# A decoder trunk's first stage reordered: second chunk later, units 0 and 1 row by row on both chunks, V's first tiles among the rows

## The chip, the cores and the metric

The kernel runs on one core of one Trainium2 chip. Five engines work from their own instruction queues: TensorE (PE, matmuls; its weight loads are PEld), VectorE (DVE), ScalarE (ACT), GpSimd (POOL) and SyncE (SP, here the issuer of most DMAs). Time is device microseconds of one execution; lower is better.

## The reference

One decoder layer for a prompt of 1024 tokens and 8 sample tokens, model width 1024, and a final norm, all in float32:

```python
mod = silu(c) @ w_ada + b_ada                       # (B, 6*D): sh1, sc1, gt1, sh2, sc2, gt2
h = rmsnorm(x, norm1_g) * (1.0 + sc1) + sh1
proj = h @ w_in                                     # xr, gr, q, k, v, o, ig, fg, u
# RG-LRU on xr, mLSTM on q k v ig fg, window pooling on u, each gated -> y_a, y_b, y_c
x = x + gt1 * (concat(y_a, y_b, y_c) @ w_out)
h2 = rmsnorm(x, norm2_g) * (1.0 + sc2) + sh2
x = x + gt2 * (square(relu(h2 @ w_ff1)) @ w_ff2)    # then the final rmsnorm
```

The change touches only the beginning: the conditioning (`mod`, of which `sh1` and `sc1` are needed first), the first norm, and the first products of `h` with `w_in`.

## The kernel before, in words

Tokens lie along the free axis. The 1032 tokens are cut into three chunks c of 344, the width 1024 into eight rows kt of 128. Float32 products are made of three fast ones: every operand is split into an upper part (`hi`, rounded by ACT) and a lower part (`lo`, the difference, made by POOL or VectorE), and TensorE adds hi\*hi, lo\*hi and hi\*lo. So each row of a 128-wide unit on one chunk is three matmuls (L2407 to L2409), a unit of eight rows 24.

`MIX_ORDER` is a text of steps, written out by hand. Every engine walks through the same list (`for s in plan`) and does its own share of each step in that order, with semaphores between the engines. So a step's place in the text sets its place on every engine that has a share in it. The steps at issue:

- `ADA:i:h`: half h of conditioning pair i (two tiles of 128 columns of `w_ada`; pieces of 512 KB that pass through four slots `RAWW`). TensorE multiplies (L2378, 8 matmuls); behind the second half ACT copies the result to `ADS` (L1297), before which it waits for the previous pair's ADT.
- `ADT:i`: TensorE turns the pair (L2392, 4 matmuls). `ADM:i`: VectorE adds the bias into `MOD` (L1717), and for the scale pairs (4 to 7) multiplies (L1719). Pair k gives the shift and pair 4+k the scale of rows 2k and 2k+1.
- `SQ:c:p`: ACT squares four rows of chunk c into two buffers (L1278), VectorE adds each to `SS` (L1763).
- `NS:c`: TensorE sums the squares over partitions (L2398, 2 matmuls), ACT takes the root (L1257), VectorE the reciprocal (L1742).
- `N:c:kt`: the normalised row. VectorE multiplies (L1728); for kt from `SHIFTED` on it adds the shift too (L1732) and ACT makes one copy to `H_hi` (L1239); for smaller kt ACT adds the shift in two operations (L1251, L1252). POOL makes `H_lo` (L1087).
- `W:u`: the weights of unit u: ACT the upper part (L1234), POOL the lower (L1082). Units 0 to 2 have early places `WR`.
- `DK:u:c:a:b`: TensorE's rows a to b-1 of unit u on chunk c, each row behind its own N. `D:u:c` for units 0 and 1 is only ACT's copy of the result.
- `WV:j`: a quarter of V's weights (784 elements a partition): ACT the upper part (L1282), VectorE the lower (L1777). `V:t`: TensorE's 24 matmuls of V on 128 tokens (L2434 to L2436), VectorE's copies (L1785, L1786); the first waits for all four WV.
- `R:n`: a DMA issue on ACT's queue.

SP issues the conditioning pieces in order (n = 0, 1, ...), the piece n behind the use of piece n-4; `SP_AFTER` says behind which piece the chunks of x (x1, x2), the early weights (w0, w1, w2) and V's weights (wv) are asked for. All through, transfers are served roughly in the order of their issue.

`bank_uses` gives each small result a PSUM bank: NS:1 had X2, which V:1 uses too.

Of the kernel before, what the change touches and what calls it, by code (L numbers as in the profile page):

```python
# [63 lines left out]
POOL_FIN = 2  # L64
POOL_STORED = (4, 6)
N_SP_RAW = 2 * len(ADA_START) + RAW
SP_AFTER = {3: ("x1",), 10: ("w1", "w0",), 16: ("wv",), 17: ("w2",), 18: ("x2",)}
N_EARLY_W = 3
R0 = NADA - N_EARLY_W


# [16 lines left out]
def unit_of(kind, t):  # L88
# [1 line left out]


MIX_ORDER = """
ADA:0:0 ADA:0:1 SQ:0:0 ADA:4:0 ADA:4:1 SQ:0:1 SQ:1:0 ADT:0 ADM:0 ADA:1:0 SQ:1:1 ADA:1:1 ADT:4 ADM:4 NS:0
ADA:5:0 ADA:5:1 N:0:0 ADT:1 ADM:1 N:0:1 ADA:2:0 ADA:2:1 ADT:5 ADM:5 ADA:6:0 ADA:6:1 ADT:2 ADM:2 N:0:2 ADA:3:0 W:0
    ADA:3:1 ADT:6 N:0:3 W:1 ADM:6 ADA:7:0 ADA:7:1 ADT:3 N:0:4 N:0:5 ADM:3 ADT:7 ADM:7 N:0:6 N:0:7 NS:1
DK:0:0:0:6
WV:0 DK:1:0:0:6
DK:0:0:6:8
WV:1 WV:2 DK:1:0:6:8
ADA:8:0  # L100
D:0:0 WV:3
D:1:0 N:1:0 N:1:1 N:1:2 N:1:3 N:1:4 V:0 SQ:2:0 DK:0:1:0:1
DK:1:1:0:1
DK:0:1:1:2
N:1:5 DK:1:1:1:2
DK:0:1:2:3
N:1:6 N:1:7 DK:1:1:2:3
DK:0:1:3:4
DK:1:1:3:4
SQ:2:1 DK:0:1:4:5  # L110
DK:1:1:4:5
R:20 ADA:8:1 DK:0:1:5:6
V:1 DK:1:1:5:6
NS:2
ADT:8 DK:0:1:6:7
DK:1:1:6:7
DK:0:1:7:8
V:2 DK:1:1:7:8
D:0:1
D:1:1 N:2:8 N:2:0 R:21 N:2:1 N:2:2 N:2:3 N:2:4 N:2:5 N:2:6 V:3 V:4 ADM:8 DK:0:2:0:8  # L120
N:2:7 W:2 V:5
D:0:2 R:22 DK:1:2:0:8
ADA:9:0 ADA:9:1 R:23 V:6 V:7 W:3 V:8 R:25 ADT:9
D:1:2 ADM:9 ADA:10:0 G1 ADA:10:1
# [73 lines left out]
def bank_uses(plan):  # L198

    count = {b: 0 for b in AUX}  # L200
    use = {}

    def add(key, bank):
        use[key] = (bank, count[bank])
        count[bank] += 1

    for s in plan:
        k = s[0]
        if k == "NS":
            add(s, ("X0", "X2", "X0")[s[1]])  # L210
        elif k == "V":
            add(s, ("X1", "X2")[s[1] % 2])
        elif k == "ADA" and s[2] == 0:
            add(("ADA", s[1]), "X3" if s[1] in ADA_START[::2] else "X4")
        elif k == "ADT":
            add(s, "X1" if s[1] in ADA_START else "X4" if s[1] == NPAIR - 1 else "X3")
        elif k in ("G1", "G2", "G3", "G4", "Y", "YS"):
            add(s, "X3")
        elif k == "TS":
            for w in range(2):  # L220
                add(("TS", w), ("X3", "X4")[w])
        elif k == "LRUG":
            for g in range(2):
                for c in range(NCH):
                    add((*s, g, c), ("X0", "X1", "X2")[c])
        elif k == "S":
            add(("S", s[1]), "X0")
            add(("KT", s[1]), "X3")
        elif k == "AB":
            add(("A", s[1]), "X1")  # L230
            add(("B", s[1]), "X2")
        elif k == "U":
            add(s, "X0")
# [56 lines left out]
def build(nc, I, O):  # L290
# [24 lines left out]
    with ExitStack() as ctx:  # L315
# [762 lines left out]
        def _(pool):  # L1078
# [25 lines left out]
            for s in plan:  # L1104
                k = s[0]
                if k == "W":
                    if s[1] < N_EARLY_W:
                        w_lo(s[1], None, s[1] % 2, WR[s[1]])
                    else:
                        w_lo(s[1], raw_slot(s[1]), s[1] % 2)  # L1110
                elif k == "N":
                    lo(full_at[s], *views(s))
                elif k == "D":
                    if s in full_at:
                        lo(full_at[s], *views(s))
                elif k in ("YD", "YSD"):
                    if k == "YD" and s[1] == 0:
                        pool.wait_ge(s_out, 32)
                    key = (k[:-1], *s[1:])
                    lo(full_at[key], *views(key))  # L1120
                elif k == "POOLY":
                    key = ("POOL", *s[1:])
                    lo(full_at[key], *views(key))
                elif s == ("POOLV", 0):

                    pool.wait_ge(h_ready, LRU_T)
                    for c in range(NCH):
# [85 lines left out]
        def _(act):  # L1213
# [30 lines left out]

            def hi_norm(n, hi_v, lo_v, fu_v, shift, kt):

                if kt >= SHIFTED:
                    hi(n, hi_v, fu_v)
                else:
                    act.wait_ge(full_ready, n + 1)  # L1250
                    nc.scalar.activation(hi_v, fu_v, ACT.Identity, bias=MOD[:, shift + kt, 0:1])  # L1251
                    nc.scalar.activation(fu_v, fu_v, ACT.Identity, bias=MOD[:, shift + kt, 0:1]).then_inc(hi_ready, 1)  # L1252
# [424 lines left out]
        def _(dve):  # L1677
# [78 lines left out]
            for s in plan:  # L1756
# [1129 lines left out]
```

## Time and profile before

| | us |
|---|---|
| median of 3 runs | 1175.13 |
| range of the runs | 1174.47 to 1175.67 |
| the profiled execution | 1175.78 |
| its span | 1174.0 |
| TensorE busy | 1124.6 (96%) |
| VectorE busy | 792.8 (68%) |
| ACT busy | 473.4 (40%) |
| POOL busy | 346.9 (30%) |
| mean granted TensorE clock | 0.982 |

The page gives the span and each engine's busy time. In the timelines a row is: start in us, length in us, engine, line of the kernel, operation, output and inputs by the program's names (buffer numbers left out), form, count, and in brackets the idle time ahead of it and who ended it. Matmuls overlap in the pipeline: one of 344 columns is shown as 0.32 us long, but the next starts 0.157 us behind it at the full clock. The granted clock (PEclk) is 1.00 for 2.4 GHz and 0.50 for 1.2 GHz.

### The profile page before, as it was taken

Reading aid. Unit: us, or ns where it says so; the run is one execution under the profiler, and the core shown is the slowest. Engines: PE = TensorE matmul, PEld = TensorE weight load, DVE = VectorE, ACT = ScalarE, POOL = GpSimd, SP = SyncE. Lnnn points to the kernel's source line nnn. Section 1 sums busy time; section 2 is a strip of 40 time slices with the busy share of each in tenths; the row PEclk is TensorE's granted clock in tenths of the full one; section 3 lists DMA queues with packets and bytes.
Section 4 is the critical chain, followed back from the end, with each engine's and each line's share of the span. In section 5 each row is a group of like instructions: output and inputs, shape, how many; then the busy total and the mean of one; then the engine's idle time right before and its main releaser. Section 6 shows DMA issues by size and latency. Waiting matters only on the chain.

```text
span 1174.0 us, 19681 instructions
## 1 busy us (share of the span) xinstructions
PE 1124.6 (96%) x7237; PEld 1077.3 (92%) x7237; DVE 792.8 (68%) x1319; ACT 473.4 (40%) x780; POOL 346.9 (30%) x275
## 2 busy tenths in 40 slices
PE   4799999999989999999999999999999999999997
PEld 1598888888979999899999999999999999999996
DVE  4561455478775434678578878778778788788546
ACT  5551355655456344642233332332432433433431
POOL 0442011201434357764032022132131231231352
PEclk9699999998989999999999999999999999999998
DMA  8912523566523722111111111202102202111104
GB/s 302 326 57 88 142 90 126 177 180 218 176 87 113 269 90 73 54 55 37 37 36 55 54 37 55 71 18 71 56 16 75 68 18 72 53 50 58 37 1 145
DMA packets 67846, 109.85 MB, mean 94 GB/s; under 512 B 6435, under 2 KB 42567, under 8 KB 67399
## 3 DMA queue, kind: packets, MB, share of 16 engines
q1 hardware_dynamic: 57574, 84.88, 22.0%
q10 hardware_dynamic: 10208, 24.12, 6.6%
q8 instruction: 41, 0.67, 0.2%
q14 instruction: 23, 0.18, 0.0%
HBM read 96.81 MB, written 12.18 MB: 93 GB/s over the span
## 4 chain that ended last, share of the span: by engine, by line
PE 82%; DVE 9%; ACT 3%; DMA 2%; issue 1%; POOL 1%; SPq 1%; ACTq 0%; POOLq 0%; DVEq 0%
PE D L2407 7%; PE D L2409 7%; PE D L2408 7%; PE D L2591 6%; PE D L2593 5%; PE D L2592 5%; PE X L2593 5%; PE X L2591 5%; PE X L2592 5%; PE X L2663 5%; PE X L2664 5%; PE X L2665 5%; PE D L2663 2%; PE D L2665 2%; PE D L2664 2%; DMA RAWW<-in_WADA 2%
## 5 line engine op out<-in xcount | busy, mean ns | idle before, releaser
L2407 PE MATMUL D<-H_hi,W_hi 128*128 128x344 f32 x472 | 158.6, 336 | 3.7 <-POOL H_lo L1087 3.1
L2409 PE MATMUL D<-H_hi,W_lo 128*128 128x344 f32 x472 | 152.4, 323 | 0.0
L2408 PE MATMUL D<-H_lo,W_hi 128*128 128x344 f32 x472 | 152.4, 323 | 0.0
L1087 POOL TENSOR_TENSOR Y_lo<-FU,Y_hi 128x344 fp32r<-128x344 f32 (+3 forms) x84 | 100.1, 1194 | 154.2 <-ACT Y_hi L1521 88.5
L1082 POOL TENSOR_TENSOR W_lo<-RAWW,W_hi 128x1024 fp32r<-128x1024 f32 x25 | 61.6, 2465 | 182.5 <-ACT W_hi L1234 182.2
L1087 POOL TENSOR_TENSOR Y_lo<-EY,Y_hi 128x344 fp32r<-128x344 f32 (+1 forms) x24 | 38.3, 1598 | 216.3 <-ACT Y_hi L1521 144.5
L2407 PEld LDWEIGHTS D<-H_hi,W_hi 128*128 128x128 f32 x472 | 90.5, 192 | 11.8 <-issue 7.6
L2408 PEld LDWEIGHTS D<-H_lo,W_hi 128*128 128x128 f32 x472 | 90.3, 191 | 0.9 <-issue 0.5
L2409 PEld LDWEIGHTS D<-H_hi,W_lo 128*128 128x128 f32 x472 | 90.2, 191 | 0.0
L2215 DVE SCALAR_TENSOR_TENSOR X<-X,MOD 128x344 f32<-128x344 f32 (+1 forms) x138 | 75.7, 566 | 9.2 <-PE X L2665 9.0
L2663 PE MATMUL X<-Y_hi,W_hi 128*128 128x344 f32 x252 | 80.7, 320 | 0.0
L2664 PE MATMUL X<-Y_lo,W_hi 128*128 128x344 f32 x252 | 80.6, 320 | 0.0
L2665 PE MATMUL X<-Y_hi,W_lo 128*128 128x344 f32 x252 | 80.5, 319 | 0.0
L2017 DVE SCALAR_TENSOR_TENSOR X<-D,MOD,X 128x344 f32<-128x344 f32 (+1 forms) x72 | 41.3, 573 | 45.4 <-PE D L2593 24.7
L2407 PE MATMUL D<-Y_hi,W_hi 128*128 128x344 f32 x192 | 62.0, 323 | 1.5 <-POOL W_lo L1082 1.5
L1099 POOL TENSOR_TENSOR SS<-SS,SQ 128x344 f32<-128x344 f32 x45 | 43.3, 963 | 65.9 <-ACT SQ L1430 40.5
L1087 POOL TENSOR_TENSOR Y_lo<-KEPT,Y_hi 128x344 fp32r<-128x344 f32 x24 | 26.4, 1098 | 120.7 <-ACT Y_hi L1521 120.7
L2408 PE MATMUL D<-Y_lo,W_hi 128*128 128x344 f32 x192 | 61.3, 319 | 0.0
L2409 PE MATMUL D<-Y_hi,W_lo 128*128 128x344 f32 x192 | 61.3, 319 | 0.0
L1556 ACT ACTIVATE W_hi<-RAWW 128x1024 fp32r<-128x1024 f32 x30 | 31.8, 1059 | 64.3 <-PE X L2665 55.6
L2378 PE MATMUL X<-RAWW,CTX 128*32 128x256 f32 x384 | 35.7, 461 | 19.5 <-DMA RAWW<-in_WADA 19.4
L1087 POOL TENSOR_TENSOR H_lo<-FU,H_hi 128x344 fp32r<-128x344 f32 (+2 forms) x33 | 29.9, 914 | 66.2 <-ACT FU L1252 50.7
(416 smaller groups left out, 3455.1 us busy)
## 6 DMA issues: line engine op xcount, KB each, us to landing
RAWW<-in_W SPq DMA_DIRECT2D x76, 512.0 KB, 3.6
RAWW<-in_WADA ACTq DMA_DIRECT2D x28, 512.0 KB, 4.1
RAWW<-in_WADA SPq DMA_DIRECT2D x20, 512.0 KB, 8.0
RAWW<-in_W ACTq DMA_DIRECT2D x18, 512.0 KB, 3.7
X0T<-in_x SPq DMA_DIRECT2D x3, 1376.0 KB, 12.8
out_y<-OUTN SPq DMA_DIRECT2D x24, 172.0 KB
X<-in_x SPq DMA_DIRECT2D x8, 344.0 KB, 5.3
NM<-nm_d SPq DMA_DIRECT2D x8, 256.0 KB, 5.3
```

The source lines that it names most:

```text
L1082: nc.gpsimd.tensor_tensor(lo_v, RAWW[:, raw, :] if src is None else src[:], hi_v.bitcast(F32), ALU.subtract).then_inc(w_lo_ready, 1)
L1087: nc.gpsimd.tensor_tensor(lo_v, fu_v, hi_v.bitcast(F32), ALU.subtract).then_inc(lo_ready, 1)
L2215: V.scalar_tensor_tensor(out=X[:, m, c * CH:c * CH + w], in0=ps[:, 0:w], scalar=MOD[:, 5 * KT + m, 0:1], in1=X[:, m, c * CH:c * CH + w], o ...
L2407: T.matmul(out, w_h, hi[:, kt, a:b], start=(kt == 0), stop=False)
L2408: T.matmul(out, w_h, lo[:, kt, a:b], start=False, stop=False)
L2409: one = T.matmul(out, w_l, hi[:, kt, a:b], start=False, stop=(kt == KT - 1))
L2591: T.matmul(out, w_h, hi(kt), start=(kt == 0 and not onto), stop=False, skip_group_check=onto)
L2592: T.matmul(out, w_h, lo(kt), start=False, stop=False, skip_group_check=onto)
L2593: one = T.matmul(out, w_l, hi(kt), start=False, stop=(kt == n - 1), skip_group_check=onto)
L2663: T.matmul(bank[:, 0:CH], w_hi[:, a:a + P], h, start=(start and k == 0), stop=False, skip_group_check=onto)
L2664: T.matmul(bank[:, 0:CH], w_hi[:, a:a + P], l, start=False, stop=False, skip_group_check=onto)
L2665: one = T.matmul(bank[:, 0:CH], w_lo[:, a:a + P], h, start=False, stop=(stop and k == 1), skip_group_check=onto)
```

## The change

The order of the first stage is rewritten; the amount of work is the same.

```diff
-SP_AFTER = {3: ("x1",), 10: ("w1", "w0",), 16: ("wv",), 17: ("w2",), 18: ("x2",)}
+SP_AFTER = {5: ("w0",), 7: ("w1",), 9: ("x1",), 15: ("wv",), 17: ("x2",), 18: ("w2",)}
 N_EARLY_W = 3
+N_DVE_W = 2
...
-ADA:0:0 ADA:0:1 SQ:0:0 ADA:4:0 ADA:4:1 SQ:0:1 SQ:1:0 ADT:0 ADM:0 ADA:1:0 SQ:1:1 ADA:1:1 ADT:4 ADM:4 NS:0
-ADA:5:0 ADA:5:1 N:0:0 ADT:1 ADM:1 N:0:1 ADA:2:0 ADA:2:1 ADT:5 ADM:5 ADA:6:0 ADA:6:1 ADT:2 ADM:2 N:0:2 ADA:3:0 W:0
-    ADA:3:1 ADT:6 N:0:3 W:1 ADM:6 ADA:7:0 ADA:7:1 ADT:3 N:0:4 N:0:5 ADM:3 ADT:7 ADM:7 N:0:6 N:0:7 NS:1
-DK:0:0:0:6
-WV:0 DK:1:0:0:6
-DK:0:0:6:8
-WV:1 WV:2 DK:1:0:6:8
-ADA:8:0
-D:0:0 WV:3
-D:1:0 N:1:0 N:1:1 N:1:2 N:1:3 N:1:4 V:0 SQ:2:0 DK:0:1:0:1
+ADA:0:0 ADA:0:1 SQ:0:0 ADA:4:0 ADT:0 ADM:0 ADA:4:1 SQ:0:1 ADA:1:0 ADT:4 ADM:4 NS:0 ADA:1:1 W:0 N:0:0 N:0:1 ADA:5:0 ADT:1 ADM:1
+ADA:5:1 W:1 ADA:2:0 ADT:5 ADM:5 DK:0:0:0:2 N:0:2 N:0:3 ADA:2:1 DK:1:0:0:2 ADA:6:0 ADT:2 ADM:2 ADA:6:1 DK:0:0:2:4
+    ADA:3:0 ADT:6 ADM:6 N:0:4 N:0:5 SQ:1:0 DK:1:0:2:4 ADA:3:1 ADA:7:0 ADT:3 ADM:3 SQ:1:1 DK:0:0:4:6 ADA:7:1 ADT:7 ADM:7 N:0:6 N:0:7 DK:1:0:4:6 NS:1
+DK:0:0:6:7
+DK:1:0:6:7 N:1:0
+DK:0:0:7:8 N:1:1
+DK:1:0:7:8
+D:0:0 WV:0
+D:1:0 N:1:2 WV:1 ADA:8:0 DK:0:1:0:1
 DK:1:1:0:1
-DK:0:1:1:2
-N:1:5 DK:1:1:1:2
-DK:0:1:2:3
-N:1:6 N:1:7 DK:1:1:2:3
-DK:0:1:3:4
+N:1:3 WV:2 DK:0:1:1:2
+DK:1:1:1:2
+N:1:4 WV:3 DK:0:1:2:3
+DK:1:1:2:3
+N:1:5 V:0 DK:0:1:3:4
 DK:1:1:3:4
-SQ:2:1 DK:0:1:4:5
+N:1:6 DK:0:1:4:5
 DK:1:1:4:5
+N:1:7 V:1
 R:20 ADA:8:1 DK:0:1:5:6
-V:1 DK:1:1:5:6
-NS:2
-ADT:8 DK:0:1:6:7
+SQ:2:0 DK:1:1:5:6
+DK:0:1:6:7
 DK:1:1:6:7
-DK:0:1:7:8
-V:2 DK:1:1:7:8
-D:0:1
-D:1:1 N:2:8 N:2:0 R:21 N:2:1 N:2:2 N:2:3 N:2:4 N:2:5 N:2:6 V:3 V:4 ADM:8 DK:0:2:0:8
-N:2:7 W:2 V:5
+SQ:2:1 DK:0:1:7:8
+DK:1:1:7:8
+D:0:1 ADT:8
+D:1:1 V:2 NS:2 N:2:8 N:2:0 R:21 N:2:1 N:2:2 V:3 N:2:3 N:2:4 N:2:5 N:2:6 V:4 N:2:7 ADM:8 DK:0:2:0:8
+W:2 V:5
...
-            add(s, ("X0", "X2", "X0")[s[1]])
+            add(s, ("X0", "X3", "X0")[s[1]])
...
-    SHIFTED = KT - 2
+    SHIFTED = ((1, 3, 5, 7, KT), (KT - 2, KT - 1, KT))
...
-                    if s[1] < N_EARLY_W:
+                    if s[1] < N_DVE_W:
+                        pass
+                    elif s[1] < N_EARLY_W:
...
-                if kt >= SHIFTED:
+                if kt in SHIFTED[shift > 0]:
...
-                    if kt >= SHIFTED:
+                    if kt in SHIFTED[shift > 0]:
...
+                elif k == "W" and s[1] < N_DVE_W:
+                    u = s[1]
+                    dve.wait_ge(w_hi_ready, u + 1)
+                    V.tensor_tensor(W_lo[:, u, :], WR[u][:], W_hi[:, u, :].bitcast(F32), ALU.subtract).then_inc(w_lo_ready, 1)
```

In words: x1 is asked for behind piece 9 instead of piece 3, w0 and w1 behind pieces 5 and 7, wv behind 15. Units 0 and 1 take chunk 0's rows in pairs between the conditioning pieces and chunk 1's rows one by one. V:0 stands before row 3 of chunk 1, V:1 before row 5, V:2 behind the chunk; the four WV stand between the N steps of chunk 1. The lower parts of W:0 and W:1 move from POOL to VectorE. In the first norm the odd rows, not rows 6 and 7, have their shift on VectorE. NS:1 gets bank X3.

## Rows read from the trace of the kernel before

**Rows 1.** The page, busy time and share of the span by engine.
```profile
PE 1124.6 (96%) x7237; PEld 1077.3 (92%) x7237; DVE 792.8 (68%) x1319; ACT 473.4 (40%) x780; POOL 346.9 (30%) x275
```
**Rows 2.** TensorE by stretches: stretch, us, busy (instructions), granted clock, DMA share, GB/s.
```profile
0.00:46.08 46.08, 24.33 (x164) 0.82 0.88 310
...
61.62:66.35 4.73, 4.73 (x31) 1.00 0.12 42
66.35:80.80 14.45, 13.05 (x81) 1.00 0.14 51
81.00:1174.00 1093.00, 1067.53 (x6883) 0.99 0.26 83
```
**Rows 3.** TensorE's waits, 0 to 81 us: total, times, longest.
```profile
PE X L2378 <- DMA RAWW<-in_WADA: 19.4, 8, 10.4
```
**Rows 4.** TensorE's timeline.
```profile
22.23 0.99 PE L2392 MATMUL X<-SEL,ADS 128*128 128x9 f32 x4 [0.34 <-DVE MOD L1717]
23.07 1.49 PE L2398 MATMUL X<-SS,ONE 128*128 128x344 f32 x2
...
35.68 1.08 PE L2378 MATMUL X<-RAWW,CTX 128*32 128x256 f32 x8 [4.77 <-DMA RAWW<-in_WADA]
...
47.45 0.49 PE L2407 MATMUL D<-H_hi,W_hi 128*128 128x344 f32 x1
47.74 0.49 PE L2408 MATMUL D<-H_lo,W_hi 128*128 128x344 f32 x1
...
55.57 0.32 PE L2409 MATMUL D<-H_hi,W_lo 128*128 128x344 f32 x1
57.24 0.45 PE L2434 MATMUL X<-WV_hi,H_hi 128*128 128x392 f32 x1 [0.78 <-DVE WV_lo L1777]
...
69.01 0.34 PE L2434 MATMUL X<-WV_hi,H_hi 128*128 128x392 f32 x1
...
73.24 0.32 PE L2407 MATMUL D<-H_hi,W_hi 128*128 128x344 f32 x1
```
**Rows 5.** ACT's timeline.
```profile
25.29 0.55 ACT L1257 ACTIVATE SS<-X,EPT 128x344 f32<-128x344 f32 x1
...
39.60 1.04 ACT L1234 ACTIVATE W_hi<-WR 128x1024 fp32r<-128x1024 f32 x1
...
49.19 2.34 ACT L1282 ACTIVATE WV_hi<-WV_raw 128x784 fp32r<-128x784 f32 x3
54.98 0.46 ACT L1322 ACTIVATE ST<-D 128x344 f32<-128x344 f32 x1 [3.45 <-PE D L2409]
...
57.71 0.58 ACT L1251 ACTIVATE H_hi<-FU,MOD 128x344 fp32r<-128x344 f32 x1 [1.18 <-DVE FU L1728]
...
58.67 0.57 ACT L1251 ACTIVATE H_hi<-FU,MOD 128x344 fp32r<-128x344 f32 x1
```
**Rows 6.** VectorE's timeline.
```profile
17.28 2.21 DVE L1763 TENSOR_TENSOR SS<-SS,SQ 128x344 f32<-128x344 f32 x4 [1.35 <-ACT SQ L1278]
...
41.13 1.99 DVE L1719 SCALAR_TENSOR_TENSOR MOD<-MOD,COLS 128x18 f32<-128x18 f32 x1
...
46.34 0.57 DVE L1728 SCALAR_TENSOR_TENSOR FU<-X0T,MOD,X 128x344 f32<-128x344 f32 x1
...
47.27 0.57 DVE L1728 SCALAR_TENSOR_TENSOR FU<-X0T,MOD,X 128x344 f32<-128x344 f32 x1
...
49.32 2.31 DVE L1742 RECIPROCAL X<-SS 128x344 f32<-128x344 f32 x1 [0.99 <-ACT SS L1257]
...
56.21 0.98 DVE L1777 TENSOR_TENSOR WV_lo<-WV_raw,WV_hi 128x784 fp32r<-128x784 f32 x1 [1.80 <-ACT WV_hi L1282]
...
63.07 2.57 DVE L1763 TENSOR_TENSOR SS<-SS,SQ 128x344 f32<-128x344 f32 x4 [0.48 <-ACT SQ L1278]
```
**Rows 7.** POOL's timeline.
```profile
40.72 2.37 POOL L1082 TENSOR_TENSOR W_lo<-WR,W_hi 128x1024 fp32r<-128x1024 f32 x1
...
58.85 4.72 POOL L1087 TENSOR_TENSOR H_lo<-FU,H_hi 128x344 fp32r<-128x344 f32 x5 [8.86 <-ACT FU L1252]
```

## The prediction

> **What bounds the kernel now.** I read the page's busy shares first: TensorE is busy 1124.6 of 1174.0 us [rows 1], so time can only come out of its idle time, of what it runs at the half clock, or be lost as new idle time. The stretches come next [rows 2]: up to 46.08 us TensorE is busy 24.3 us, with the DMA queues at 0.88 of their share (the conditioning weights stream in); from 57.24 on it is busy nearly all the time at the granted clock 1.00. Past 81 us nothing of the order changes and TensorE works 1067.5 of 1093 us, so what the first 81 us lose or gain goes through to the end almost one to one. Of TensorE's waits in these 81 us 19.4 us are for conditioning pieces [rows 3]; for V's weights it waits 0.78 us, ahead of V:0 [rows 4]. The timelines [rows 4 to 7] give the durations. I use one marker: at 80.80 us before, TensorE has finished units 0 and 1 on chunks 0 and 1, V:0 to V:2, both halves of ADA:8, ADT:8 and NS:2. The new order contains the same work up to a point behind D:1:1; I ask when that point comes.
>
> **Part 1, the start up to NS:0 (gain about 4 us, hidden later).** Before, ADT:4 waited for ADM:0, which VectorE did behind chunk 1's first squares (the row at 22.23, [rows 4]); NS:0 followed at 23.07. Chunk 0's squares were summed at 17.28 + 2.21 = 19.5 [rows 6]. With ADM:0 ahead of SQ:0:1, and chunk 1's squares gone, NS:0 starts at 19.5 and takes 1.4; the root 0.55 [rows 5] and the reciprocal 2.31 [rows 6] end at 23.9, where before the root began at 25.29 and the reciprocal ended at 28.2. Asking for x1 six pieces later moves 1.41 MB, at 310/0.88 = 352 GB/s [rows 2] 4.0 us of the queues, but the bytes ahead of the last piece (ADA:7:1) are the same, so I take nothing from that by itself.
>
> **Part 2, chunk 0 among the pieces (over at about 51 us, before at 55.9, [rows 4]).** All engines follow the same order, so each pair of rows waits for a chain: piece, ACT's copy, ADT, ADM, N, ACT, POOL.
> - Rows 0 and 1: W:0's low part on VectorE, 0.98 x 1024/784 = 1.27 us (estimate from the 784-wide row in [rows 6]), 23.9 to 25.2; N:0:0 0.5, N:0:1 0.93 with its shift (46.34 to 47.27 in [rows 6]): 26.6. ACT 0.55 behind, POOL 0.92 each (4.72/5, [rows 7]): first dense row on TensorE at 28.7.
> - Rows 2 and 3: ACT's copy for ADA:5 0.4 and W:1's upper part 1.04 [rows 5] end at 28.6; VectorE's W:1 1.27, ADM:5 0.4, two N 1.43: 31.7. ACT is free for ADA:2's copy at 32.3, done at 32.7.
> - TensorE from 28.7: at the half clock a DK of two rows is 6 x 0.287 = 1.72 (47.45 to 47.74, [rows 4]), a piece 1.0 to 1.08, an ADT 1.0. DK, ADA:2:1, DK end at 33.1. Wide matmuls take most of this stretch, as in the one before the clock's rise at 50 us, so I let the clock be full from about 33. Then ADA:6:0, ADT:2, ADA:6:1, DK, ADA:3:0, ADT:6 at half those durations: 3.6, so 36.7.
> - ADM:6 0.4, N:0:4 and N:0:5 1.43, ACT 0.55: 39.3. Now ACT does SQ:1:0 before it copies ADA:3, and SQ:1:1 before it copies ADA:7. Four squares with their sums take 2.21, and 2.57 where POOL works on rows beside them (17.28 and 63.07, [rows 6]); I take 2.6. 39.3 + 2.6 + 0.4 + 2.6 + 0.4 = 45.3. ADT:7 0.7, ADM:7 0.4, two N 1.45, ACT 0.5, root 0.55, reciprocal 2.35: chunk 1's reciprocal ends at 51.3.
>
> Call that moment T; before it was 49.32 + 2.31 = 51.6 [rows 6]. So T hardly moves, though chunk 0's dense work is over by then. Bounds: with the full clock from 28.7, ADT:2 is held by ACT's copy at 32.7 and T is 50.0. With the half clock throughout, TensorE needs 6 x 1.72 + 7 x 1.0 + 4 x 1.0 + 1.4 = 22.7 us from 28.7 and some 0.7 of waits, and T is 52.1 + 0.55 + 2.35 = 55.0. I take 51.4.
>
> **Part 3, V's weights split between the rows (the loss).** Before, WV:0 to WV:2 stood together on ACT (2.34 for three) and on VectorE, and ran under the 9.8 us of chunk 0's dense work (46.1 to 55.9); only WV:3 waited (for the ACT copy of D:0:0 at 54.98), and V:0 started at 57.24 [rows 4 to 6]. Now the order on ACT and on VectorE alike is WV:0, N:1:2, WV:1, N:1:3, WV:2, N:1:4, WV:3. A WV goes from ACT to VectorE and an N from VectorE to ACT. So ACT can't start WV:1 before VectorE has done N:1:2, and VectorE can't start N:1:3 before ACT has done WV:1. Nothing overlaps. One round is WV on ACT 0.78 (2.34/3), 0.12, WV on VectorE 0.98, N on VectorE 0.5 or 0.93, 0.1, N on ACT 0.96 or 0.47 (57.71 to 58.67 in [rows 5]; a shifted row is the single copy): 3.4 us. From T: N:1:0 to ACT and its two ACT operations 1.6, N:1:1 on ACT 0.47, D:0:0's copy 0.4, WV:0 0.78, that is 3.25; three rounds to WV:3's ACT part, 10.2; 0.12 + 0.98. V:0 may start at T + 14.6 = 66.0.
>
> Until then TensorE has ADA:8:0 and three double rows of chunk 1, 6 x 0.157 = 0.94 each (4.73/30, [rows 2]), and stands behind V:0, which comes before row 3. It is idle from about 59 to 66, and sparsely used from 51 on. So the cover that is gone is chunk 0's dense work: it was over V's weights and chunk 1's normalising, and has been spent on the piece waits.
>
> From V:0 to the marker: three V tiles at 73.24 - 69.01 = 4.23 [rows 4], 12.7; five double rows, 4.7; and the rest of the stretch 66.35 to 80.80, 13.05 - 8.46 - 18 x 0.157 = 1.8 (ADA:8:1, ADT:8, NS:2). Sum 19.2. Row 7 of chunk 1 and SQ:2 are done while V:1 runs, so no wait there. 66.0 + 19.2 = 85.2.
>
> **Part 4, the clock behind the hole.** Before, the dense work began at 46.1 and still ran at half speed at 47.7 (0.29 us a matmul against 0.157, [rows 2, 4]); about twelve of its matmuls were slow, which cost 12 x 0.13 = 1.6 us. Behind an idle stretch of 7 us V:0 will start at half speed as well: 0 to 2.5 us, I take 1.7.
>
> **Part 5, chunk 2.** NS:2 now stands behind V:2. V:3 and V:4 (8.5 us) cover 12.5 us of root, reciprocal and nine rows at POOL's 0.92 less 3.3 us of dense rows in progress: 0.3 us more wait than before, 0 to 1.0.
>
> **Part 6, W:0 and W:1 off POOL, odd shifts on VectorE.** The MOD operation that takes 0.2 us otherwise took 1.99 while POOL's 2.37 us W operation ran, and ended with it [rows 6, 7]. That goes, and is in T. The 4.7 us of POOL were otherwise not on the path. The odd shifts make a row 0.47 on ACT and 0.93 on VectorE where it was 0.96 and 0.5: in a serial round that is nothing. The same row says that VectorE's WV operations, which now fall among POOL's row operations, can be held by them: at worst 0.92 each, 3.7 for four. In the round above POOL's row operation starts together with ACT's WV of 0.78 and is nearly over when VectorE's turn comes, so the sum takes nothing and the worst is a rival.
> The Trainium skill, "SBUF — State Buffer", section "Who interferes with whom", says that a VectorE operation with two SBUF inputs and a GpSimd operation that reads SBUF lock each other out for a whole instruction, whichever is issued first. By that each of the three rounds grows by the end of POOL's operation that overlaps, some 0.2 us, and the sum by 0.6; by the row alone it could be nothing or all of it.
>
> **Sum.** 85.2 + 1.7 + 0.3 = 87.2 against 80.8: +6.4 us, I say +6.2, since a little may be taken up by later waits. The profiled execution took 1175.78 us (span 1174.0), 0.65 over the median of 1175.13. So 1182.0 for such an execution, 1181.3 for a median. Own range: T 50.0, no clock cost: 64.6 + 19.2 = 83.8, +3.0; T 55.0 with 2.5 and 1.0: 69.6 + 19.2 + 3.5 = 92.3, +11.5, which all three bounds rarely reach together. 1178 to 1186.5.
>
> **Rivals.**
> - Faster: the rows fill the piece waits and chunk 1's chain comes forward with NS:0. Chunk 0's 9.5 us shrink to its last two double rows at 1.9: -7.6 us, +1.0 for a late first row of chunk 1, so 1175.1 - 6.6 = 1168.5. For it speaks that 19.4 us of piece waits are there to be filled, and that NS:0 comes 4.4 us sooner. Against it: V:0 would have to start before 66.0 - 6.2 = 59.8, T + 14.6 says T at 45.2, and the two square groups on ACT between ADA:3 and ADA:7 alone put ADT:7 behind 45. 0.10.
> - No change: the hole behind T is only as long as what was saved, which asks for T near 45. 1175.1. 0.04.
> - The lock of part 6 or a late clock makes it worse: POOL's operations hold each WV by 0.92, 1181.3 + 3.7 = 1185.0. 0.06.
> - That the second chunk, asked for late, holds SQ:1:0: it would have to land after 39; with the pieces before it, it lands near 30. It is in none of the sums, under 0.01.
>
> My forecast holds 0.80. Faster by over 0.2% 0.10, within 0.2% (2.3 us, about what a measurement of this kernel can tell from none) 0.04, slower 0.86. The range is stretched downward to 1176 for the part between.
>
> **What would show it.** NS:0's reciprocal ends near 24, the one of NS:1 near 51. On VectorE and ACT WV and N alternate with about 3.4 us from one WV to the next. TensorE waits some 6 to 7 us for WV_lo ahead of V:0 at about 66, with the clock at 0.5 in this stretch; the marker stands at 87. It is wrong if NS:1's reciprocal ends by 46, or if WV:3's low part is done by 60.

## The result and the profile after

The changed kernel takes 1184.0 us (median of 7 runs, 1182.6 to 1188.06), the one before 1175.47 beside it (7 runs, 1172.84 to 1179.29). The ratio is 1.0087, 95% interval 1.0067 to 1.0107: slower by 0.9%. Forecast was 1181.3 in a range of 1176.0 to 1186.5.

| | before | after |
|---|---|---|
| profiled execution, us | 1175.78 | 1184.0 |
| its span | 1174.0 | 1182.2 |
| TensorE busy | 1124.6 | 1124.8 |
| mean granted clock | 0.982 | 0.983 |
| chunk 1's reciprocal ends (T) | 51.63 | 54.69 |
| V:0 starts | 57.24 | 69.18 |
| marker: V:0 to V:2, both units on two chunks, NS:2 done | 80.80 | 90.38 |
| second marker, see below | 116.92 | 127.85 |

TensorE is as busy as before over the whole span; what is new is idle time. The page of the kernel after, busy time by engine (answers to [rows 1]):

```profile
PE 1124.8 (95%) x7237; PEld 1076.3 (91%) x7237; DVE 794.3 (67%) x1327; ACT 470.5 (40%) x774; POOL 341.9 (29%) x273
```

TensorE by stretches (stretch, us, busy, granted clock, DMA share, GB/s; answers to [rows 2]):

```profile
42.00:52.50 10.50, 8.52 (x32) 0.53 1.02 381
52.50:62.50 10.00, 5.42 (x36) 0.98 0.23 80
62.50:73.00 10.50, 4.29 (x16) 0.53 0.01 2
73.00:90.38 17.38, 17.38 (x107) 0.99 0.15 54
```

Two stretches ran at half speed (1.2 GHz), and from 52.5 to 73.0 TensorE did only 9.7 us of work. Before, the corresponding time behind T was nearly full: 17.8 of the 20 us from 52 to 72. TensorE's waits in the first 100 us (waiting tile, releaser, total, times, longest; answers to [rows 3]):

```profile
PE X L2384 <- DMA RAWW<-in_WADA: 12.9, 6, 10.1
PE X L2440 <- DVE WV_lo L1783: 6.2, 1, 6.2
PE X L2398 <- ACT ADS L1299: 5.9, 3, 3.8
PE D L2413 <- POOL H_lo L1087: 4.8, 3, 2.4
PE X L2404 <- DVE SS L1765: 0.9, 1, 0.9
```

The piece waits did shrink, from 19.4 to 12.9 us, but 6.2 us for V's weights (0.8 before), 5.9 for ACT's copies (none before) and 4.8 for chunk rows (1.8 before) have come instead. TensorE's timeline (answers to [rows 4]):

```profile
19.08 1.51 PE L2404 MATMUL X<-SS,ONE 128*128 128x344 f32 x2 [0.94 <-DVE SS L1765]
...
43.15 1.02 PE L2398 MATMUL X<-SEL,ADS 128*128 128x9 f32 x4 [3.78 <-ACT ADS L1299]
44.02 0.63 PE L2413 MATMUL D<-H_hi,W_hi 128*128 128x344 f32 x1
...
46.02 1.08 PE L2384 MATMUL X<-RAWW,CTX 128*32 128x256 f32 x8
47.67 1.02 PE L2398 MATMUL X<-SEL,ADS 128*128 128x9 f32 x4 [0.56 <-ACT ADS L1299]
...
50.41 1.35 PE L2404 MATMUL X<-SS,ONE 128*128 128x344 f32 x2
...
57.52 0.40 PE L2413 MATMUL D<-H_hi,W_hi 128*128 128x344 f32 x1 [2.43 <-POOL H_lo L1087]
61.79 0.40 PE L2413 MATMUL D<-H_hi,W_hi 128*128 128x344 f32 x1 [2.15 <-POOL H_lo L1087]
69.18 0.69 PE L2440 MATMUL X<-WV_hi,H_hi 128*128 128x392 f32 x1 [6.21 <-DVE WV_lo L1783]
...
73.27 0.37 PE L2440 MATMUL X<-WV_hi,H_hi 128*128 128x392 f32 x1
...
104.02 0.43 PE L2413 MATMUL D<-H_hi,W_hi 128*128 128x344 f32 x1 [0.94 <-POOL H_lo L1087]
```

In VectorE's timeline (answers to [rows 6]) the four WV operations stand apart, each behind a wait for ACT's part, and N operations between them (the third, at 64.70, is left out):

```profile
52.38 2.31 DVE L1744 RECIPROCAL X<-SS 128x344 f32<-128x344 f32 x1 [1.66 <-ACT SS L1259]
...
57.88 1.20 DVE L1783 TENSOR_TENSOR WV_lo<-WV_raw,WV_hi 128x784 fp32r<-128x784 f32 x1 [1.67 <-ACT WV_hi L1284]
61.43 1.04 DVE L1783 TENSOR_TENSOR WV_lo<-WV_raw,WV_hi 128x784 fp32r<-128x784 f32 x1 [1.87 <-ACT WV_hi L1284]
...
68.09 1.04 DVE L1783 TENSOR_TENSOR WV_lo<-WV_raw,WV_hi 128x784 fp32r<-128x784 f32 x1 [1.87 <-ACT WV_hi L1284]
```

The chain of waits that ended last shows the same as one thread (start, us, what). One round, from N:1:2 to WV:1:

```profile
59.08 0.49 DVE FU L1730
59.58 0.03 issue
59.60 0.58 ACT H_hi L1253
60.19 0.47 ACT FU L1254
60.66 0.76 ACT WV_hi L1284
61.41 0.02 issue
61.43 1.04 DVE WV_lo L1783
```

No piece of it lies on two engines at once. The waits in the timelines say the same: VectorE stood 1.87 us for ACT ahead of its operation at 61.43 (above), and ACT stood 1.41 us for VectorE ahead of its own at 59.60:

```profile
59.60 0.58 ACT L1253 ACTIVATE H_hi<-FU,MOD 128x344 fp32r<-128x344 f32 x1 [1.41 <-DVE FU L1730]
```

That is the round of part 3.

### The profile page after: what moved, and what is told of

Its sections match the earlier page's. It is cut to its first block, busy times and chain, and to the rows that moved or that the text cites. A ratio compares the mean times of both kernels' runs of the same rounds, so it can differ in the third digit from the quotient of the medians.

```text
span 1182.2 us, 19690 instructions
## 1 busy us (share of the span) xinstructions
PE 1124.8 (95%) x7237; PEld 1076.3 (91%) x7237; DVE 794.3 (67%) x1327; ACT 470.5 (40%) x774; POOL 341.9 (29%) x273
## 4 chain that ended last, share of the span: by engine, by line
PE 80%; DVE 10%; ACT 3%; DMA 3%; issue 1%; POOL 1%; SPq 1%; POOLq 0%; ACTq 0%; DVEq 0%
PE D L2413 7%; PE D L2415 6%; PE D L2414 6%; PE D L2597 6%; PE D L2599 5%; PE D L2598 5%; PE X L2599 5%; PE X L2597 5%; PE X L2598 5%; PE X L2669 5%; PE X L2671 5%; PE X L2670 5%; PE D L2669 2%; PE D L2671 2%; PE D L2670 2%; DMA RAWW<-in_WADA 2%
## 5 line engine op out<-in xcount | busy, mean ns | idle before, releaser
L1082 POOL TENSOR_TENSOR W_lo<-RAWW,W_hi 128x1024 fp32r<-128x1024 f32 x25 | 61.3, 2452 | 179.7 <-ACT W_hi L1236 179.3
L2413 PEld LDWEIGHTS D<-H_hi,W_hi 128*128 128x128 f32 x472 | 90.5, 192 | 19.2 <-issue 13.7
L2414 PE MATMUL D<-Y_lo,W_hi 128*128 128x344 f32 x192 | 61.3, 319 | 0.0
L2415 PE MATMUL D<-Y_hi,W_lo 128*128 128x344 f32 x192 | 61.3, 319 | 0.0
L1558 ACT ACTIVATE W_hi<-RAWW 128x1024 fp32r<-128x1024 f32 x30 | 31.7, 1058 | 63.9 <-PE X L2671 55.3
L2671 PEld LDWEIGHTS X<-Y_hi,W_lo 128*128 128x128 f32 x252 | 47.4, 188 | 0.0
```

Of the source, the lines that this page charges most:

```text
L1082: nc.gpsimd.tensor_tensor(lo_v, RAWW[:, raw, :] if src is None else src[:], hi_v.bitcast(F32), ALU.subtract).then_inc(w_lo_ready, 1)
L2413: T.matmul(out, w_h, hi[:, kt, a:b], start=(kt == 0), stop=False)
L2414: T.matmul(out, w_h, lo[:, kt, a:b], start=False, stop=False)
L2415: one = T.matmul(out, w_l, hi[:, kt, a:b], start=False, stop=(kt == KT - 1))
L2671: one = T.matmul(bank[:, 0:CH], w_lo[:, a:a + P], h, start=False, stop=(stop and k == 1), skip_group_check=onto)
```

## How the experiments are read

The executions of one kernel differ by 2 to 9 us, so besides the timed ratio I use a place in the order that every kernel has: the first matmul that turns V's gate columns (`X<-IDN,GTE`), which stands behind all that the change moves. It is the second marker of the table, 116.92 us before and 127.85 after (+10.9). Its row in TensorE's timeline, in the kernel before:

```profile
116.92 0.27 PE L2458 MATMUL X<-IDN,GTE 128*36 128x128 f32 x1 [0.29 <-DVE MOD L1717]
```

In the kernel after:

```profile
127.85 0.27 PE L2464 MATMUL X<-IDN,GTE 128*36 128x128 f32 x1 [0.29 <-DVE MOD L1719]
```

The kernel before was profiled a second time (before_again):

> The kernel before, unchanged, profiled once more. It tells how far one trace of a kernel stands from another. Theory (the first stage is the same from execution to execution within 2 us, which is set by where the clock rises, and the spread of the times comes from the half-clock stretches between 240 and 365 us): matmul 1200 starts within 2 us of 214.4 and the rest of the span differs by 0 to 4 us with the half-clock time. Rival (the first stage itself varies by 3 us or more): the differences of 4 us that the experiments' traces show would not be safe.

There the marker is at 116.43, 0.5 us from the first profile, although the whole execution took 1178.25 us instead of 1175.78. The kernel both, profiled twice, had it 0.9 us apart. So the first stage repeats better than the total, but a difference of 1 to 2 us at the marker, which rests on one trace on either side, is only a little more than that. Three of the recorded expectations speak of matmul 1200 of the trace instead; it stands at 214.4 us in the kernel before and moves as the marker does (10.9 us later in the kernel after). All kernels, in us:

| kernel | T | marker, against before | span, against before | ratio to before | 95% |
|---|---|---|---|---|---|
| after | 54.7 | +10.9 | +8.2 | 1.0087 | 1.0067 to 1.0107 |
| wv_together | 54.3 | +6.7 | +10.2 | 1.0076 | 1.0052 to 1.0100 |
| v_behind_rows | 55.0 | +9.6 | +9.5 | 1.0083 | 1.0064 to 1.0101 |
| squares_early | 50.1 | +6.0 | +4.7 | 1.0052 | 1.0033 to 1.0070 |
| both | 50.1 | +2.7 | +5.9 | 1.0063 | 1.0044 to 1.0083 |
| both_again (one execution) | 51.4 | +3.6 | +7.1 | | |
| x1_early | 56.2 | +13.4 | +10.4 | 1.0111 | 1.0084 to 1.0139 |
| w_on_pool | 55.1 | +12.5 | +15.9 | 1.0080 | 1.0055 to 1.0105 |
| before_dve_w | 53.5 | +2.2 | +0.2 | 1.0032 | 1.0016 to 1.0047 |
| covered | 53.5 | -4.0 | -5.4 | 0.9959 | 0.9944 to 0.9974 |
| covered_wv14 | 53.3 | -4.1 | +1.1 | 0.9949 | 0.9929 to 0.9969 |
| rows_late | 51.5 | -2.3 | -0.5 | 1.0004 | 0.9987 to 1.0021 |
| before_again (one execution) | 50.8 | -0.5 | +2.4 | | |

## The experiments

**wv_together.** The changed kernel with V's weights in one piece.

```diff
-D:0:0 WV:0
-D:1:0 N:1:2 WV:1 ADA:8:0 DK:0:1:0:1
+D:0:0 WV:0 WV:1 WV:2 WV:3
+D:1:0 N:1:2 ADA:8:0 DK:0:1:0:1
 (and WV:2, WV:3 gone from behind N:1:3 and N:1:4)
```

> The changed kernel with its four WV steps together behind D:0:0, where only WV:0 stood; all else as changed. Theory (serial rounds): T, the end of chunk 1's reciprocal, stays at 54.7. ACT does four WV in a row from 57.0 (0.78 each), VectorE follows with the last at about 61.1 to 62.0, then N:1:2. TensorE waits for row 2 of chunk 1 until about 64.3 and goes straight on to V:0 there, instead of 69.2: 4.9 us less, and up to 1.5 more because the clock has less idle time to fall in. Ratio to the kernel before about 1.003 instead of 1.0087. Rival (V's weights are late for another reason, their transfer or POOL's hold on VectorE): V:0 still starts at 68 to 69 and the time is that of the changed kernel.

VectorE's timeline of wv_together, where the four now run back to back:

```profile
57.45 3.85 DVE L1783 TENSOR_TENSOR WV_lo<-WV_raw,WV_hi 128x784 fp32r<-128x784 f32 x4 [1.67 <-ACT WV_hi L1284]
```

They are done at 61.3 instead of 69.1; V:0 starts at 65.86 and waits for nothing, TensorE's longest wait is 3.8 us for a row of chunk 1 instead of 6.2 for the weights. The marker comes 4.2 us sooner than in the kernel after. So the serial rounds are a cause, and one edit of the order on ACT and VectorE takes 4.2 of the 10.9 us away. The total doesn't show it: 1.0076, which is 1.3 us under the changed kernel's 1.0087 and inside both intervals. Where the rest went is taken up in the part on the total below.

**v_behind_rows.** V:0 moved behind row 4 of chunk 1, so that TensorE meets it later.

```diff
-N:1:5 V:0 DK:0:1:3:4
+N:1:5 DK:0:1:3:4
...
-N:1:7 V:1
+V:0 N:1:7 V:1
```

> The changed kernel with V:0 behind row 4 of chunk 1 on all engines instead of ahead of row 3; the WV stay between the N. Theory (serial rounds): rows 3 and 4 come no faster than one per 3.4 us (ready at 64.9 and 68.3), so they only fill the wait: V:0 starts at about 69.3 as before, two double rows of 0.94 are already done, 1.9 us less, perhaps 1 more by the clock. Ratio 1.006 to 1.007. Rival (V:0's place ahead of the rows makes the loss, the rows are ready): TensorE's wait of 6.2 us goes altogether and the ratio is 1.003 or less.

The marker is 1.3 us sooner, against the 1.9 and perhaps 1 more that were expected. WV_lo starts at 58.22, 61.77, 65.03 and 68.42, 3.3 to 3.6 us apart as in the kernel after: TensorE's order has no part in the rounds. It only decides how many rows are used to fill the hole, and there are few to be had, since the rows' own N operations stand in the same rounds.

**squares_early.** Chunk 1's squares before the last pieces instead of between them.

```diff
-... ADT:2 ADM:2 ADA:6:1 DK:0:0:2:4
-    ADA:3:0 ADT:6 ADM:6 N:0:4 N:0:5 SQ:1:0 DK:1:0:2:4 ADA:3:1 ADA:7:0 ADT:3 ADM:3 SQ:1:1 ...
+... ADT:2 SQ:1:0 ADM:2 ADA:6:1 DK:0:0:2:4 SQ:1:1
+    ADA:3:0 ADT:6 ADM:6 N:0:4 N:0:5 DK:1:0:2:4 ADA:3:1 ADA:7:0 ADT:3 ADM:3 ...
```

> The changed kernel with SQ:1:0 ahead of ADM:2 and SQ:1:1 ahead of ADA:3:0, so chunk 1's squares lie in ACT's and VectorE's idle time at 32 to 38 us. Theory (T is set by the squares between ACT's copies of ADA:3 and ADA:7): ADT:3 starts at about 41 instead of 43.15, ADM:7 ends at 45 to 46 instead of 49.2, T is 50 to 51.5 instead of 54.7, V:0 starts 14.5 later at 65 to 66: 3 to 4 us less, ratio 1.005. Rival (the clock or the pieces set T): T stays within 1 us of 54.7.

TensorE and VectorE of squares_early:

```profile
41.03 0.61 PE L2398 MATMUL X<-SEL,ADS 128*128 128x9 f32 x4 [1.77 <-ACT ADS L1299]
...
64.57 0.69 PE L2440 MATMUL X<-WV_hi,H_hi 128*128 128x392 f32 x1 [5.33 <-DVE WV_lo L1783]
```
```profile
47.77 2.31 DVE L1744 RECIPROCAL X<-SS 128x344 f32<-128x344 f32 x1 [1.01 <-ACT SS L1259]
```

ADT:3 waits 1.77 us instead of 3.78 for ACT's copy, the clock stays at 1.00 from 42 to 52 us, where the kernel after had 0.53, and T is 50.08, 4.6 sooner. V:0 starts at T + 14.5, as in the kernel after. The marker is 5.0 sooner, more than the 3 to 4 expected, and the time follows it (1.0052). That the edit keeps the clock full is not shown: see both_again.

**both.** The two edits together, timed, and **both_again**, the same kernel profiled a second time.

> The changed kernel with the edits of wv_together and squares_early at once. Each took 4.2 and 4.9 us off the stage (matmul 1200 of the trace came 10.9 us later than before in the changed kernel, 6.7 and 6.0 later in these two). Theory (serial rounds and T are two losses one behind the other): they add up, 10.9 - 4.2 - 4.9 = 1.8 us later than before, ratio 1.000 to 1.004. Rival (both took off the same idle time): 5 us or more later, 1.005.

> The kernel both, unchanged, profiled once more. Its trace showed the stage 2.7 us longer than before, but its times were 7.4 us longer. Theory (clock): matmul 1200 again 1 to 4 us later than the kernel before; the rest is half-clock time behind 240 us, which differs from execution to execution. Rival (the stage of that one trace was a lucky one): matmul 1200 comes 5 us or more later.

At the marker the edits roughly add up: -4.2 and -5.0 from +10.9 give +1.8, measured +2.7 and +3.6. The total doesn't: 1.0063 is 7.4 us, its interval (5.2 to 9.8 us) doesn't hold the marker's figure, and the ratio expected, at most 1.004, was missed.

The two profiles of this one kernel also price the clock by itself. TensorE from 42 to 52 us (columns as above), in both, then in both_again:

```profile
42.00:52.00 10.00, 6.45 (x45) 1.00 1.02 387
```
```profile
42.00:52.00 10.00, 9.17 (x35) 0.53 1.04 385
```

ADT:3 waited 1.76 us in the first and 1.61 us in the second; ADT:7 started at 44.11 and 44.40, NS:1 at 45.61 and 47.14, and T is 50.07 and 51.41. So the half clock in this stretch costs T 1.3 us, or 2.0 counted from ADT:3, which began at 41.02 and 40.37, and the same order gave it in one execution and not in the other. By this estimate 1.3 to 2.0 of the 4.6 us by which squares_early has T sooner are the clock, and the rest is the squares' place.

**x1_early.** The changed kernel with x1 asked for behind piece 3 again.

```diff
-SP_AFTER = {5: ("w0",), 7: ("w1",), 9: ("x1",), 15: ("wv",), ...
+SP_AFTER = {3: ("x1",), 5: ("w0",), 7: ("w1",), 15: ("wv",), ...
```

> The changed kernel with the second chunk of x asked for behind piece 3 as before; all else as changed. Theory: its 1.4 MB then stand ahead of pieces 4 to 9, ADA:1:0 starts at about 19.5 instead of 16.1, NS:0 behind it at about 21 instead of 19.1, and ADA:1:1 and all that follows some 2 to 3.5 us later: T at 57 to 58, the stage 2 to 3.5 us longer, ratio 1.011. Rival (the request's place is free, since the bytes ahead of the last piece are the same): stage within 0.5 us of the changed kernel.

Piece waits rise from 12.9 to 15.0 us, chunk 0's reciprocal ends at 25.90 instead of 23.59, and the marker is 2.5 us later (ratio 1.0111). So asking for the second chunk late is worth 2.5 us at the marker in this order: an early x1 holds the pieces in front of NS:0, where ADA:1:0 starts at 19.52 behind a wait of 3.44 us, instead of at 16.09. The timed ratios, 1.0111 and 1.0087, have intervals that overlap.

**w_on_pool** and **before_dve_w.** The lower parts of W:0 and W:1 back on POOL in the changed kernel (`N_DVE_W = 0`); and, alone, in the kernel before, moved to VectorE with the odd rows shifted there.

> The changed kernel with the lower parts of W:0 and W:1 back on POOL. In the kernel before, the move of these two to VectorE (with the odd shifts) made the stage 2.2 us longer. Theory (in the new order POOL is idle at 23 to 26 and 28 to 31, so it makes no difference where they run; N:0:0 starts 1.2 us sooner, ADM:5 is held until POOL's W ends, some 1 us later): stage within 1 us of the changed kernel, ratio to the kernel before 1.008 to 1.009. Rival (VectorE is too loaded and this is part of the loss): 2 us or more less, 1.007 or below.

> The kernel before with only two parts of the change: the lower parts of W:0 and W:1 on VectorE, and the odd rows of the first norm with their shift on VectorE. Theory: no share in the loss; the VectorE operation on MOD that took 1.99 us goes back to 0.2, the two W take 1.25 each there; time within 1 us of the kernel before (ratio 0.999 to 1.001). Rival (these parts cost: VectorE is loaded where it is on the path): 1.002 or more.

In the changed kernel POOL's version puts the marker 1.5 us later and the ratio (1.0080) can't be told from 1.0087. There VectorE's operation on MOD for ADM:5 takes 2.02 us again (at 28.10, beside POOL's operation for W:1). In the kernel before, VectorE's version, together with the odd shifts, costs 2.2 us at the marker and 0.32% in time, which I had not expected. VectorE of before_dve_w:

```profile
43.81 1.23 DVE L1780 TENSOR_TENSOR W_lo<-WR,W_hi 128x1024 fp32r<-128x1024 f32 x1 [1.50 <-ACT W_hi L1237]
44.95 0.17 DVE L1720 TENSOR_TENSOR MOD<-X,COLS 128x18 f32<-128x18 f32 x1
```

VectorE, which walks the order too, stands 2.07 us (at W:0) and 1.50 us (at W:1) waiting for ACT's upper part, and ADM:6 behind it comes at 44.95 instead of 40.92. It ends at 45.34, against 43.12 in the kernel before, where POOL's operation had stretched it: 2.2 us later, which is the figure at the marker. TensorE's next ADT waits 3.0 us for it. POOL could wait for ACT with nothing behind it. How much of the 2.2 us the odd shifts have was not tested apart. It is the same effect as in the rounds: an added hand-over stops everything that the receiver has further on.

**covered.** A version of my own: both squares early; WV:0 to WV:2 behind ADM:3 while chunk 0 is still being worked on, WV:3 behind NS:1, wv asked for behind piece 13; V:0 and V:1 right behind chunk 0's rows, ahead of chunk 1's dense rows. Further on NS:2 stands ahead of row 6, and V:2 to V:4 among chunk 2's N steps. It shows what these edits do together, not what each of them does.

```diff
-...ADA:7:0 ADT:3 ADM:3 SQ:1:1 DK:0:0:4:6 ADA:7:1...
-DK:1:0:6:7 N:1:0
-D:0:0 WV:0
-D:1:0 N:1:2 WV:1 ADA:8:0 DK:0:1:0:1
+...ADA:7:0 ADT:3 ADM:3 WV:0 WV:1 WV:2 DK:0:0:4:6 ADA:7:1...
+WV:3 DK:1:0:6:7 N:1:0
+D:0:0
+D:1:0 N:1:2 ADA:8:0 N:1:3 V:0 N:1:4 N:1:5 N:1:6 N:1:7 V:1 R:20
+DK:0:1:0:1 SQ:2:0
...
```

> The change's first part kept (chunk 0's rows among the pieces, second chunk late), and its losses taken away: chunk 1's squares in the idle time at 32 to 38 us, V's weights asked for behind piece 13 and split at 41 to 45 us (WV:0 to WV:2 behind ADM:3, WV:3 behind NS:1), V:0 and V:1 straight behind chunk 0's rows as cover while chunk 1 is normalised, NS:2 ahead of row 6, V:2 to V:4 as cover for chunk 2. Theory (the loss is serial rounds without cover plus T): chunk 0 done near 50, V:0 from 51, no wait for chunk 1's rows, the 450th matmul some 6 to 8 us sooner than before: 1167 to 1170, ratio 0.993 to 0.995. Rival (the opening is bound by its pieces, and chunk 0's rows among them gain nothing): no faster than the kernel before, ratio 1.00.

TensorE of covered:

```profile
41.28 0.79 PE L2385 MATMUL X<-RAWW,CTX 128*32 128x256 f32 x8 [3.44 <-DMA RAWW<-in_WADA]
...
54.60 0.45 PE L2441 MATMUL X<-WV_hi,H_hi 128*128 128x392 f32 x1 [0.61 <-DVE WV_lo L1784]
```

V:0 starts 14.6 us sooner than in the kernel after, at once at full speed (its matmuls stand 0.18 us apart), and covers chunk 1's eight rows. The marker is at -4.0 us and the kernel is faster than the kernel before and the kernel after, 0.9959 (0.9944 to 0.9974). The expectation was a few us better. I took the row at 41.28 for what is missing, and the next run tests that: the 1.6 MB of wv now stand ahead of ADA:7:0, TensorE waits 3.44 us for it and the clock falls to 0.51 until 52.

**covered_wv14.** The same with wv one piece later.

> The kernel covered with V's weights asked for behind piece 14 instead of 13. In covered TensorE waited 3.4 us for ADA:7:0 at 41.3, whose transfer stood behind the 1.6 MB of V's weights. Theory: the wait goes, chunk 1's reciprocal ends at 50 to 51 instead of 53.5, the stage is 2 to 3.5 us shorter than covered, 6 to 7.5 us shorter than before: 1167 to 1169, ratio 0.993 to 0.995. Rival (the wait only moves to ADA:7:1, one piece later): within 1 us of covered, 0.996.

TensorE of covered_wv14:

```profile
44.68 1.08 PE L2385 MATMUL X<-RAWW,CTX 128*32 128x256 f32 x8 [1.33 <-DMA RAWW<-in_WADA]
```

The wait for ADA:7:0 is 0.77, at 39.48, and one of 1.33 stands at ADA:7:1 instead; VectorE waits 2.54 us for V's upper parts. T and marker stay where they were (53.3, -4.1), where T at 50 to 51 was expected: the rival came true. The queues were at 1.05 of their share in this stretch: I take it that V's weights and the last two pieces have to come in before T in whatever order, which no run tests apart. The ratio is 0.9949 (0.9929 to 0.9969), not to be told from covered.

**rows_late.** covered_wv14 with chunk 0's dense rows all behind NS:1, as in the kernel before.

> The kernel covered_wv14 with chunk 0's twelve DK groups behind NS:1, in the pieces' order of the kernel before (0:6, 0:6, 6:8, 6:8), so nothing dense runs among the pieces. Theory (rows among the pieces save TensorE's time once V:0 and V:1 cover the rest): the pieces come sooner without them, the last dense row of chunk 0 ends at 54 to 57 instead of 52.6 and V:0 starts there instead of at 54.4: the stage 1 to 3 us longer than covered_wv14, ratio 0.996 to 0.998. Rival (they only take time from the chain of pieces): the same or less time, 0.995 or below.

T comes 1.9 us sooner (51.45), for no dense row at half speed stands before NS:1, but all 16 rows then follow it; the marker (114.64) is 1.9 us later than in covered_wv14 (112.78). So the rows among the pieces, the main idea of the change, are a gain of 1.9 us at the marker, if nothing is spoiled behind them. The ratio is 1.0004 where 0.996 to 0.998 was expected: timed, the two kernels are about 6.5 us apart (1.0004 against 0.9949, intervals that don't touch). The sign is the marker's; the other 4.6 us lie behind it and stay open, since the one profile of either kernel doesn't show them.

## Why the prediction was right, and where its numbers were off

The sign and the mechanism held, the price of the first stage was too low, and part of the agreement in the total is luck. At the first marker it had 87.2 and the trace has 90.38; at the second the kernel is 10.9 us late, where the sum said 6.4. By its steps:

- **Part 1 held.** NS:0 started at 19.08 (19.5 said), its reciprocal ended at 23.59 (23.9).
- **Part 2 was mis-sized, by 3.3 us: T is 54.69, not 51.4.** First row and N:0:2/3 came as said (28.00 for 28.7, 31.2 for 31.7), ADM:6 was done at 38.09 (36.7 + 0.4 = 37.1 said; the sum's next figure, 39.3, should by its own terms be 39.1). Then ADT:3 had to wait for a copy behind SQ:1:0 until 43.15 (42.3 said). The step that failed is the next one: I had added up only ACT's work from SQ:1:0 to ADT:7, and let the clock be full from 33. In those 3.78 us of waiting the clock fell to half (0.53 from 42.0 to 52.5), and ADA:7:1 stood behind a double row on TensorE that started at 44.02 and took 2.0 us, so that ADA:7:1 began at 46.02, ADT:7 at 47.67 and NS:1 at 50.41. From ADT:7's start (47.67, 45.3 said) that is 2.4 us; ADT:7 at half speed adds 0.4 and ACT's root, which had to wait for NS:1, 0.5. T lies just inside my bound of 55.0, which was made of just this, the half clock on TensorE's own chain. squares_early takes the wait from 3.78 to 1.77, had the full clock and gives T = 50.08, my lower bound of 50.0. How the 3.3 us divide between the order on ACT and the clock is not shown for this kernel; both and both_again put the clock at 1.3 to 2.0 us there.
- **Part 3 held.** V:0 started at T + 14.49 (14.6 said), with rounds of 3.55, 3.27 and 3.39 us (3.4 said) and a wait of 6.2 (6 to 7 said). wv_together removes the wait and 4.2 us; v_behind_rows leaves the rounds alone.
- **Part 4 held.** The clock was 0.53 from 62.5 to 73.0, and V:0's first 12 matmuls took 73.27 - 69.18 = 4.09 us instead of 12 x 0.176 = 2.1 [rows 4]: 2.0 us (1.7 said). From V:0 to the first marker 21.2 us passed (19.2 + 1.7 said).
- **Part 5 was mis-sized, by 1.0 us.** The row behind V:4 starts at 98.93, against 89.24 in the kernel before: +9.7. From V:5 at 104.60 against 93.64 it is +11.0. In between TensorE waits for chunk 2's last rows, the longest wait being 0.94 us at 104.02 (0.36 before). I had said 0.3, within 0 to 1.0; with the 0.3 it is 1.3, above that bound.
- **Part 6.** The VectorE operation that POOL's W operation had stretched to 1.99 us takes 0.18, as said, and W:0's lower part 1.23 (1.27 said). As VectorE's WV operations stood 1.20, 1.04, 1.04 and 1.04 us, against 0.98 alone, the lock that was a rival at 3.7 us cost 0.4. By the Trainium skill, "SBUF — State Buffer", section "Who interferes with whom", VectorE is locked out for the rest of POOL's instruction. POOL's row operations ended 0.37, 0.21, 0.20 and 0.21 us behind the starts of the WV operations, 1.0 in all, so the rule gives the place and an upper bound, and the trace shows less than half of it. What I had not seen is the cost of VectorE waiting for ACT at W:0 and W:1 (before_dve_w). In the changed order ACT's part was ready at W:0 (VectorE's operation at 23.62 waits for nothing) but not at W:1, where VectorE waited 1.78 us (28.12); even so POOL's version was no better there (w_on_pool).

Together: 6.4 + 3.3 (part 2) - 0.1 (part 3) + 0.3 (V:0 to the first marker) + 1.0 (part 5) = 10.9.

The rival on the other side, the rows filling the piece waits, was half right: the piece waits fell by 6.5 us. It failed where it asked for T by 45. rows_late against covered_wv14 shows that the filling alone is worth 1.9 us; covered shows that its gain is kept once V's weights are ready and V stands where chunk 0's dense work used to be the cover.

**From the marker to the total.** The profiled execution of the kernel after is only 8.2 us longer than that of the kernel before. The rest came back mainly at 240 to 300 us, through the clock. TensorE by stretches there (columns as above), in the kernel before, then after, then both:

```profile
240.00:300.00 60.00, 57.41 (x419) 0.94 0.64 197
```
```profile
240.00:300.00 60.00, 56.18 (x431) 1.00 0.63 189
```
```profile
240.00:300.00 60.00, 57.91 (x403) 0.91 0.60 186
```

A mean clock of 0.94 over 60 us is 3.6 us of work lost, 0.91 is 5.4, and 1.00 none. Added to the markers: after 10.9 - 3.6 = 7.3 (span +8.2), both 2.7 + 1.8 = 4.5 (+5.9), both_again, also at 0.91, 3.6 + 1.8 = 5.4 (+7.1), wv_together, at 0.91, 6.7 + 1.8 = 8.5 (+10.2). In two kernels these 60 us explain less: covered, at 1.00, -4.0 - 3.6 = -7.6 (-5.4), and covered_wv14, at 0.94, -4.1 (+1.1). The second had a half-speed stretch just ahead of them:

```profile
230.00:240.00 10.00, 8.35 (x43) 0.66 0.97 294
```

Taken over everything from the marker to 380 us, by the traces' record of the granted clock, the half clock loses 3.4 us (after, x1_early, covered, before_dve_w) to 10.2 us (w_on_pool, covered_wv14) of work, and 6.8 in the kernel before. From the marker to the end the fourteen traces take 1054.1 to 1062.3 us; less that loss it is 1050.2 to 1052.3 in every one. So of the 8 us by which they differ behind the marker all but 2 are this clock. That what the first stage loses goes through one to one therefore held for the work, but not for the clock: the total of the kernel after lies nearer to the forecast than its marker because it lost 3.4 us less to the half clock than the kernel before. That was luck.

From the marker to 300 us the clock fell at two places (a further fall, beginning between 338 and 360 us, is in every trace), both at a short wait for VectorE's `EX` in the mixers' small matmuls. In TensorE's timeline of the kernel before, of after and of both, in this order, the later place:

```profile
267.82 1.41 PE L2520 MATMUL X<-VB,EX 128*128 128x97 f32 x8 [1.67 <-DVE EX L1895]
```
```profile
278.84 1.13 PE L2526 MATMUL X<-VB,EX 128*128 128x97 f32 x8 [1.44 <-DVE EX L1901]
```
```profile
272.13 1.96 PE L2526 MATMUL X<-VB,EX 128*128 128x97 f32 x8 [1.63 <-DVE EX L1901]
```

The eight matmuls take 1.13 us at full speed; where they take more the clock fell among them. It fell there in before (wait 1.67), before_again (1.95), wv_together (1.56), both (1.63), both_again (1.71), covered_wv14 (1.84), rows_late (1.54), v_behind_rows (1.35) and w_on_pool (1.16), in squares_early (1.21) 2.1 us behind, and not in after (1.44), x1_early (1.10), covered (1.07) and before_dve_w (1.70). At the wait for `EX` one round earlier, some 30 us sooner, it fell in eight traces, with waits of 1.25 us (before_dve_w) to 2.04 us (w_on_pool), and not in the other six, with waits of 0.85 us (v_behind_rows) to 1.32 us (after). Longer waits mostly go with a fall, but no length separates the two. No run changed the order there, so what decides it stays open, and with it what wv_together alone is worth in the total: -4.2 us at the marker, not shown in the ratio.

## What to carry to other kernels

When two engines walk one written order, steps handed over in opposite directions (A to B, then B to A) must not alternate: here each pair cost 3.4 us where the work of either engine was half of that, and grouping the steps took 4.2 us back at the marker. When work is moved forward to fill waits, ask what it used to cover where it stood, and put other ready work there; and a hand-over given to the engine that others wait for costs what stands behind it, not its own length. Judge an edit of a first stage by a marker in the trace that lies behind it, and by the timed ratio as well: the two can differ by what the clock does later. Profile a kernel twice before a difference of 1 to 2 us at such a marker is believed.

## What was not expected of the hardware

- The granted clock fell at waits of TensorE that were quite short. In the kernel after it was 0.53 from 42.0 to 52.5 us, from within a wait of 3.78 us, and in covered_wv14 it fell at 42.0 with waits of 0.77 and 0.78 us before it; in squares_early, with one of 1.77 us, it stayed at 1.00 there. One kernel can do either: both had 1.00 from 42 to 52 us and both_again 0.53, with waits of 1.76 and 1.61 us.
- Far behind the first stage, at 240 to 300 us, with TensorE busy for 56 to 58 of 60 us, the mean clock was 0.89 (w_on_pool) to 1.00 from kernel to kernel: 0.11 x 60 = 6.6 us of some 1175, with falls at waits of 2.04 us and less. The kernel before had 0.94 in one profile and 0.93 in the other, with a further fall at 237.8 us in the second only, and its totals differed by 2.5 us (1175.78 and 1178.25) with markers 0.5 us apart.
- VectorE's sums of squares took 2.80 us for four beside a POOL operation (40.64) where they take 2.21 alone (13.52 and 16.81).
